# Two transformer-like blocks on one core: a narrower first query tile, norms behind a first unit, and a last layer begun on half its inputs

## What is computed

```
# first block
s = q . k over the allowed keys (causal: key <= query, dilated windows)   16 heads of 64
p = softmax(s); o = p @ v          # beside it a state-space branch
x = x + concat(attn, ssm) @ w_out
x = x + cross_attention(rms_norm(x, g_cross), rms_norm(mem, g_mem))
x = x + square(relu(rms_norm(x, g_mlp) @ w_up)) @ w_down
# second block
n = rms_norm(x, attn_norm) @ w_in  # MLA, 16 heads of 128+64, causal; an RG-LRU branch; gates
h = x + (g_attn * y_attn + g_rnn * y_rnn) @ w_out
# experts: per token and head the 16 best of 16384, 8 heads: 128 rows of 2048 from two tables
h = h + sum_k gate_k * gelu(u_k . rms_norm(h, ffn_norm)) * v_k
g = sigmoid(rms_norm(h, ple_norm) @ w_ple_gate); h = h + g * (p @ w_ple_proj)
out = rms_norm(h, final_norm)
```

## Time and profile before

| what | value |
|---|---|
| median of 3 runs | 3889.14 us (3883.0 to 3893.53) |
| profiled execution, own time | 3886.61 us |
| its span | 3884.6 us |
| PE busy | 3305.3 us, 85% |
| DVE busy | 2470.6 us, 64% |
| ACT busy | 1428.7 us, 37% |
| GpSimd busy | 847.1 us, 22% |
| DMA moved | 952.98 MB |

### The profile page before, as it was taken

The page is one execution under the profiler, slowest core; times in us unless marked ns, Lnnn a source line. Parts: engine busy times, 40 slices in busy tenths (PEclk is TensorE's granted clock), DMA queues, the critical chain, the costliest instruction groups (busy, mean ns, idle before and its releaser), DMA issues.

```text
span 3884.6 us, 53098 instructions
## 1 busy us (share of the span) xinstructions
PE 3305.3 (85%) x21008; PEld 2742.1 (71%) x21008; DVE 2470.6 (64%) x3257; ACT 1428.7 (37%) x2042; POOL 847.1 (22%) x623
## 2 busy tenths in 40 slices
PE   8988998999999999999999996766666666666688
PEld 8977887999999999999998996732222223222248
DVE  6567865654455556875546666977777776555556
ACT  6555555553345444564445452221000111000124
POOL 2000011000000100000000011255665565565522
PEclk9998999999999999999999997888888888888899
DMA  6423253555556565555552455899999999999964
GB/s 231 148 98 109 96 160 110 162 185 187 183 179 190 176 200 174 163 180 184 166 179 96 157 185 213 315 355 422 421 422 422 422 422 420 421 421 421 421 260 140
DMA packets 188023, 952.98 MB, mean 245 GB/s; under 512 B 20992, under 2 KB 20992, under 8 KB 121984
## 3 DMA queue, kind: packets, MB, share of 16 engines
q0 software_dynamic: 73728, 536.90, 33.6%
q1 hardware_dynamic: 114048, 412.70, 33.0%
HBM read 947.42 MB, written 2.10 MB: 244 GB/s over the span
## 4 chain that ended last, share of the span: by engine, by line
PE 58%; DMA 18%; DVE 13%; ACT 4%; POOL 4%; issue 2%; DVEq 0%; ACTq 0%; POOLq 0%; SPq 0%
PE ps L524 58%; DMA BIG<-in_peer_v,CS 6%; DMA HLF<-in_peer_v,CS 6%; DVE HL L1748 3%; DMA HF<-in_peer_v,CS 3%; DVE BIG L1752 2%; POOL HLF L506 2%; POOL BIG L506 2%; DMA BIG<-in_peer_u,CS 2%; DVE BIG L2390 1%; DMA HLF<-in_peer_u,CS 1%; DVE BIG L1748 1%; ACT BIG L1115 1%; ACT HL L1121 1%; PE ps L528 1%
## 5 line engine op out<-in xcount | busy, mean ns | idle before, releaser
L524 PE MATMUL ps<-HS,HL 128*128 128x256 f32 x10128 | 1344.8, 288 | 36.0 <-DVE HL L1748 29.9
L524 PEld LDWEIGHTS ps<-HS,HL 128*128 128x128 f32 x10128 | 1291.8, 196 | 47.5 <-DVE HL L1748 34.7
L1748 DVE TENSOR_TENSOR HL<-RAW,HL 128x1024 fp32r<-128x1024 f32 (+1 forms) x772 | 954.6, 1237 | 237.4 <-ACT HL L1121 174.1
L1121 ACT CAST HL<-RAW 128x1024 fp32r<-128x1024 f32 (+1 forms) x772 | 805.4, 1043 | 502.1 <-PE ps L524 454.4
L524 PE MATMUL ps<-BIGR,HL 128*128 128x256 f32 x6720 | 893.3, 284 | 24.2 <-DVE HL L1748 14.8
L524 PEld LDWEIGHTS ps<-BIGR,HL 128*128 128x128 f32 x6720 | 849.0, 192 | 32.2 <-issue 14.8
L524 PE MATMUL ps<-BIG,HF 128*128 128x512 f32 (+1 forms) x760 | 398.8, 675 | 191.2 <-DMA BIG<-in_peer_v,CS 168.1
L524 PE MATMUL ps<-HLF,HF 128*128 128x512 f32 x656 | 342.5, 674 | 154.2 <-DMA HLF<-in_peer_v,CS 140.6
L524 PEld LDWEIGHTS ps<-BIG,HF 128*128 128x128 f32 (+1 forms) x760 | 161.3, 222 | 423.3 <-issue 386.0
L473 POOL COPY NSUM<-TMP 128x256 f32<-128x256 f32 x6 | 3.3, 553 | 1957.6 <-ACT TMP L1117 1957.6
L2390 DVE CUSTOM_DVE_ANT_0 BIG<-BIG 128x2048 f32<-128x2048 f32 x133 | 305.0, 2293 | 167.3 <-DMA BIG<-in_peer_u,CS 158.1
(11 more groups left out here) (194 smaller groups left out, 2235.3 us busy)
## 6 DMA issues: line engine op xcount, KB each, us to landing
RAW<-in_w_up SPq DMA_DIRECT2D x128, 512.0 KB, 4.0
RAW<-in_w_down SPq DMA_DIRECT2D x128, 512.0 KB, 4.2
RAW<-in_w_out SPq DMA_DIRECT2D x64, 512.0 KB, 4.3
RAW<-in_w_qk SPq DMA_DIRECT2D x32, 512.0 KB, 3.4
RAW<-in_w_xbc SPq DMA_DIRECT2D x32, 512.0 KB, 3.5
RAW<-in_w_xr SPq DMA_DIRECT2D x32, 512.0 KB, 3.5
RAW<-in_w_yr SPq DMA_DIRECT2D x32, 512.0 KB, 3.8
RAW<-in_w_gr SPq DMA_DIRECT2D x32, 512.0 KB, 4.4
```

The lines of the kernel that those rows point to most:

```text
L524: return e.matmul(o, l, r, start=start, stop=stop, skip_group_check=True)
L1121: s.done(e.copy(o, i), sig)
L1748: v.done(e.tensor_tensor(o, a, b, op), sig)
```

## The change

1. Causal heads: the first tile's scores are taken over the first 128 keys alone. A head's scores are now 128 + 256 = 384 columns (`CAUSAL`), and so are the mask, the masking operation and the probabilities. The maxima take two reductions.
2. The four norm seams: PE's `norm_end` is called after the first unit of the next layer; ACT's makes a one-element root (`warm`) and `high(unit0 + 3)` ahead of its wait; DVE's makes `low(unit0 + 2)` and `low(unit0 + 3)` ahead of its wait.
3. Of the last 16 v rows DVE takes those with odd k, 8 instead of 4.
4. w2_pg is in `LATE`: its first three units need chunks 0 to 7 only. DVE's order of joining, adding, low halves and units is written anew, PE's first unit comes ahead of the last two half sums, ACT makes the third unit's high half ahead of the third half square, and the fourth's after the root.
5. Output: ACT multiplies each chunk of X by the gain into OUT inside the last layer; after the reciprocal DVE does four products of 1024 columns.

```
-LATE = ("w_ck", "w_out", "w2_ao")
+LATE = ("w_ck", "w_out", "w2_ao", "w2_pg")
+CAUSAL = ((0, 128), (128, 256))
...
         def by_vector(g):
-            return g[0] == "u" or g[2] % 4 == 3
+            return g[0] == "u" or g[2] % 4 == 3 or (g[1] == 15 and g[2] % 2 == 1)
...
# PE
-            def dense(L, src, evac=None, bg=None):
+            def dense(L, src, evac=None, bg=None, norm=None):
...
                         p.then_inc(s_mm, 1)
+                        if norm is not None and u == L.unit0:
+                            norm()
...
-                    for i in range(2):
-                        p = mm(b[:, i * T:i * T + T], QK[lo:lo + 64, c, i * 128:i * 128 + 128], QK[lo:lo + 64, 8 + c, :],
+                    for i, (at, w) in enumerate(CAUSAL):
+                        p = mm(b[:, at:at + w], QK[lo:lo + 64, c, i * 128:i * 128 + 128], QK[lo:lo + 64, 8 + c, 0:w],
...
-            norm_end("g_cross")
-            dense(L["w_cq"], normed("g_cross"), evac_cq, g_cr)
+            dense(L["w_cq"], normed("g_cross"), evac_cq, g_cr, lambda: norm_end("g_cross"))
...
-            half_sum(1, 2)
-            half_sum(1, 3)
-            dense(L["w2_pg"], cut_by(hg, s_nlo, lambda k: NORMED["ple_norm"] + k + 1))
+            def later_sums():
+                half_sum(1, 2)
+                half_sum(1, 3)
+            dense(L["w2_pg"], cut_by(hg, s_nlo, lambda k: NORMED["ple_norm"] + k + 1), None, None, later_sums)
...
# ACT
+            def warm():
+                act(WARM[:, :], con("ones")[:, 0:1], ACT.Sqrt)
-            def norm_end(name):
+            def norm_end(name, L=None):
+                if L is not None:
+                    warm()
+                    high(L.unit0 + 3)
                 s.wait_ge(s_nlo, NORMED[name] + 16)
                 rstd(name, 0, ADDED[name] + 1, RX, 2048, s_nsum)
...
             for j in range(4):
+                if j == 2:
+                    high(pg.unit0 + 2)
                 half_square(1, j)
...
                 squared("final", c)
-            high(pg.unit0 + 2)
+                act(OUT[:, c, :], X[:, c, :], ACT.Identity, (s_xg, c + 1), scale=vec("final_norm", c))
+            high(pg.unit0 + 3)
             dense(pg, evac_pg)
+            warm()
...
# DVE
             def norm_end(name, L=None):
                 normed_low(name, 15)
+                if L is not None:
+                    low(L.unit0 + 2)
+                    low(L.unit0 + 3)
                 v.wait_ge(s_nfree, NORM[name] + 1)
                 recip(RX, RX, (s_rx, RXN[name]))
...
+                stt(P[:, 0:384], score_bank(k)[:, 0:384], scale, con("mask"), ALU.mult, ALU.add, sig_score(k))
+                for i, (at, w) in enumerate(CAUSAL):
+                    total(d[:, i:i + 1], P[:, at:at + w], ALU.max, True, (s_max, n + 1) if i else None)
...
+            for b in range(3):
                 joined(1, b)
+            added(1, 0)
+            joined(1, 3)
+            added(1, 1)
+            low(pg)
+            normed_lows(0)
+            added(1, 2)
+            normed_lows(1)
+            low(pg + 1)
+            added(1, 3)
+            low(pg + 2)
+            normed_lows(2)
+            normed_lows(3)
+            low(pg + 3)
...
-            for c in range(16):
-                stt(OUT[:, c, :], X[:, c, :], vec("final_norm", c), RS[:, 0, :], ALU.mult, ALU.mult,
+            for i in range(4):
+                o = OUT[:, 4 * i:4 * i + 4, :]
+                tt(o, o, RS[:, 0, :].unsqueeze(1).to_broadcast([128, 4, T]), ALU.mult, (s_pout, i + 1))
```

More of the change, by code:

```diff
@@ L217, in build @@
         NSUM = sb("NSUM", [128, T])
+        WARM = sb("WARM", [128, 1])
         RX, CX = KEEP[:, 2, :], KEEP[:, 3, :]
@@ L649, in prepared, with softmax_head @@
                     yield
-            def softmax_head(name, h, score, P, PT, causal, vl, lo, rows, ahead=2):
+            def softmax_head(name, h, score, P, PT, vl, lo, rows, ahead=2):
                 k = SCORE[name] + (MLAH[h] if name == "mla" else h)
@@ L659, in softmax_head @@
                 pe.wait_ge(s_tfree, t)
-                for j, (i, c) in enumerate([(0, 0), (1, 0), (1, 1)] if causal else [(0, 0), (1, 0), (0, 1), (1, 1)]):
-                    p = tr(tr_bank[:, j * 128:j * 128 + 128], P[:, i * T + c * 128:i * T + c * 128 + 128])
+                for j in range(3):
+                    p = tr(tr_bank[:, j * 128:j * 128 + 128], P[:, j * 128:j * 128 + 128])
                 p.then_inc(s_turn, 1)
@@ L686, in attn @@
                     bank_done(L["w_v"], 7)
-                yield from softmax_head("attn", h, score, AP_[h % 4], APT, True,
+                yield from softmax_head("attn", h, score, AP_[h % 4], APT,
                                         lambda kt: VT[:, kt, h * 64:h * 64 + 64], lo, 64, 3)
@@ L982, in value @@
                     return V2[kt][:, h * 128:h * 128 + 128]
-                yield from softmax_head("mla", h, score, MP[h % 3], MPT, True, value, 0, 128)
+                yield from softmax_head("mla", h, score, MP[h % 3], MPT, value, 0, 128)
             g_ml = pipeline(mla(h) for h in range(16))
@@ L1036, in evac_pq @@
                 pq[0] = c + 1
-            dense(L["w_pq"], normed("ffn_norm"), evac_pq, beside())
+            dense(L["w_pq"], normed("ffn_norm"), evac_pq, beside(), lambda: norm_end("ffn_norm"))
             drain(g_sc)
@@ L1219, in prepared, with softmax_head @@
                     yield
-            def softmax_head(name, h, P, PT, scale, masked, causal, o, lo, rows, ahead=2):
-                k, n = SCORE[name] + (MLAH[h] if name == "mla" else h), HEAD[name] + h
+            def softmax_head(name, h, P, PT, o, lo, rows, ahead=2):
+                n = HEAD[name] + h
                 s.wait_ge(s_max, n + 1)
[L1224 to L1233, removed]
+                d = den(h)
+                for i, (at, w) in enumerate(CAUSAL):
+                    act(P[:, at:at + w], P[:, at:at + w], ACT.Exp, (s_exp, EXP[name] + h + 1) if i else None,
+                        bias=d[:, i:i + 1], acc=d[:, 2 + i:3 + i])
                 for _ in range(ahead):
                     yield
-                t, w = TURN[name] + h, 384 if causal else 512
+                t = TURN[name] + h
                 s.wait_ge(s_turn, t + 1)
@@ L1632, in scalar @@
             dense(L["w2_out"], residual("ffn_norm", L["w2_out"]))
-            norm_end("ffn_norm")
+            norm_end("ffn_norm", L["w_pq"])
             def rows():
@@ L2523, in constants @@
     m = ((d >= 0) & (d <= 128)).astype(int) + ((d >= 0) & (d % 4 == 0)) + ((d >= 0) & (d % 16 == 0))
-    c["mask"] = np.where(m > 0, np.log(np.maximum(m, 1)), NEG).reshape(128, 512)
+    c["mask"] = causal(np.where(m > 0, np.log(np.maximum(m, 1)), NEG))
     c["iota"] = np.broadcast_to(np.arange(16), (128, 16))
@@ L2540, in constants2 @@
     trig = np.stack([np.cos(ang), np.sin(ang)], axis=1).astype(np.float32)
-    return trig, np.where(d >= 0, 0.0, NEG).reshape(128, 512).astype(np.float32)
+    return trig, causal(np.where(d >= 0, 0.0, NEG)).astype(np.float32)
 def kernel(**inp):
```

95 lines of the change are left out of this document (37 added, 58 removed).

## The result

The changed kernel took 3862.7 us (median of 4 runs, 3859.9 to 3863.0) against 3887.9 us for the kernel before on the same chip (3883.0 to 3893.5): a ratio of 0.9933, 95% interval 0.9916 to 0.9950, so 0.7% faster, and clear of the spread. The forecast was 3856 with a range of 3844 to 3868. The time lies in the range and the direction was right, but the profiled span fell by 23.6 us (3884.6 to 3861.0) where the sum said 32.3.

The account below looks back on a forecast made before the run. TensorE was taken to bound the dense layers and DMA the expert gathers between them. Terms 3.0 + 6.7 + 13.2 + 6.2 + 3.2 = 32.3 us, from the median of 3889.14 to 3856.8, stated as 3856; range 3844 to 3868.

Parts of the forecast that it names:

- Narrow tile, attention: Attention stage: first query tile scored against 128 keys instead of 256 saves 3.0 us, bounds 1 to 4.5.
- Narrow tile, MLA: MLA stage: the narrower first-tile scores save TensorE 6.7 us, all taken as gain, bounds 4 to 7.5.
- Seams: Four norm seams: cross 2.6, MLP 3.0, attn_norm 5.1, ffn_norm 2.5; together 13.2 us, bounds 10 to 18.
- rival on the clock: The rival that the seams give the clock back: gain 36.5 us, up to 40, time 3851; chance 0.12.
- Rows: Last 16 expert rows: TensorE does 8 instead of 12, VectorE's joining starts at 3753.6; gain 3.75 us.
- the clock falls between the rows: Rival: TensorE's last eight expert rows run slow, and attention's chains surface; gain 24 us, time 3865; chance 0.17.
- the rows' stage absorbs it: Rival: the expert rows' stage ends at a fixed time, losing 22.9 us of earlier gains; time 3880; chance 0.03.
- Last layer: Last layer started on half its inputs: with the rows' 3.75 us a gain of 6.2, bounds 4.3 to 8.
- slower: Rival: the clock stays low through the last layer's 748 fast matmuls, ending 37 us slower, 3926; chance 0.02.
- Output: Kernel's end: sixteen VectorE products become four of 1024 columns; gain taken as 3.2 us, bounds 2.4 to 3.4.
- The seams give the clock back: Rival: no low clock at the seams; MLP gives 5.4 us, last layer up to 8; time 3851; chance 0.12.
- likeliest case: Whole kernel: the forecast itself, all terms together giving 32.3 us and a time of 3856; chance 0.66.

Follow-up runs that it names:

- both_wide: both_first, but MLA's first query tile scored against 256 keys on TensorE again; 3855.6 us, ratio 0.9923.
- both_first: The changed kernel with VectorE and TensorE serving MLA's newest live head first instead of the oldest; 3850.6 us, ratio 0.9908.
- fill_head12: The changed kernel with seven unused constant matmuls (3.0 us) on TensorE ahead of its wait at MLA's head 12; 3857.7 us, ratio 0.9925.
- seams_only: The kernel before with the four norm seam edits alone; 3876.7 us, ratio 0.9976.
- narrow_only: The kernel before with the narrow first query tiles of attention and MLA alone; 3877.4 us, ratio 0.9977.
- pe_first: The changed kernel with TensorE alone serving MLA's newest head first; 3858.2 us, ratio 0.9927.

## Why the prediction was right, and where it failed

**Narrow tile, attention.** Forecast 3.0. The pair of traces shows 2.0, ten executions with the narrow tile and three without differ by 4.3 on average at g_cross's last add (602.6 against 606.9). Inside my bounds of 1 to 4.5, and not to be had more exactly: this stretch differs by up to 2.5 us between executions of like code.

**Narrow tile, MLA.** This is the step that failed: "In MLA PE waited 1.7 us in 200, so I take all 6.7." The size of PE's saving was right (0.42 us a head, and both_wide against both_first gives 6.70). But the wait was read as a small remainder of idle, and so as proof that PE is the bound. It was the opposite: the one place where PE's lead over a slower ring comes due. PE had run ahead of the ring by 0.2 us a head for the whole stage; making it faster by 0.42 only spent the lead sooner. The ring itself gained 0.19 us a head, 3 us in all, and the wait grew from 1.74 to 3.26. Then the clock fell and took 3.8 us more, so that MLA gave -1.2 us from the first value product to the last (91.97 to 93.18), and 0.0 from its first score. With the clock kept up (fill_head12) the same stretch takes 105.4 us against 109.3. So of the 6.7 us the clock took 3.9 and the ring kept back 2.8. I had written that "a chain through DVE and ACT may surface", but with a lower bound of 4, where nothing was possible; and of the clock only in other places.

**Seams.** Forecast 13.2; 13.3 in seams_only. In the changed kernel cross gave 3.7 instead of 2.6: PE's first scores of cross came 2.2 us sooner, counted from g_cross's last add, and they ran at the full clock, where the kernel before had the low one. PE's timeline, before and changed:

```profile
633.50 2.04 PE L524 MATMUL ps<-BIG 128*128 128x256 f32 x4 [1.29 <-DVE BIG L1748]
...
629.30 1.10 PE L529 MATMUL ps<-BIG 128*128 128x256 f32 x4 [1.29 <-DVE BIG L1755]
```

This isn't chance: these matmuls take 1.10 us in all ten kernels with the seam edit and 2.04 or 2.05 in the three without, and the whole stretch 84.3 to 85.5 us against 88.4 to 89.1. It belongs to my rival on the clock. The low clock moved more than it went: it was at 0.50 from 632.9 to 639.7 and again from 653.4 to 660.2 us in the kernel before, from 641.5 to 655.2 in the changed one. attn_norm gave about 4.3 instead of 5.1: its first four units met no idle, but the fifth waited 0.89 us for its low, where I had no wait. The MLP gave 2.6 instead of 3.0. So the sum agrees because the misses cancel. The 2.98 us of idle at the MLP and the place of the reciprocal ahead of the routing came as forecast. DVE's reciprocal of ffn_norm at 2330.34 is 12.5 us sooner than in the earlier trace rows, the transposes 15.2.

**Rows.** Forecast 3.75, found 3.7 in all nine kernels that have the edit. Of PE's eight last rows in the changed kernel six followed 1.15 to 1.31 us of idle and took 3.67 us; the first followed 3.79 us of idle and was slow, as in the kernel before, and the second came behind it without idle, which the forecast's "eight PE rows" with 1.3 us of idle overlooked. The rival "the clock falls between the rows" is refuted. So is "the rows' stage absorbs it": from the routing's transposes to DVE's last row it took 1393.0 to 1396.6 us wherever it began, from 2329 to 2357 us. One count of mine was short: over the whole stage of the kernel before 60 rows, not 35, followed 3.77 us of idle or more; all of them were slow.

**Last layer.** Forecast 2.45, found 2.1. The waits that I had laid out came where I had put them: for the fourth half sum's square (1.27 us) and for the fifth low (1.72). The rival "slower", with the clock low in the last layer, didn't occur; from 3748 us it is 1.00.

**Output.** Forecast 3.2, found 3.1.

**The seams give the clock back** came true in part: the sum's matmul takes 0.60 us at three seams, at two of which (attn_norm and ffn_norm) it had taken 1.22, and cross ran faster than forecast. But the clock that was lost at MLA's end is more than what was given back.

So the likeliest case was right in all terms but one; taking out its 7.5 us leaves a gain of 24.8 and a forecast of 3864.3 on the median's scale, where 3862.7 was measured. The range held because it reached to the low ends of the bounds.

## What to carry to other kernels

In a stage that several engines pass work round in turn, measure the pace of each: the time from one head to the next of one operation on each engine, and how the distance between two engines' operations drifts along the stage. A single wait at the stage's end, small against the stage, doesn't show that the waiting engine is the bound; where the distance shrinks steadily, it isn't. There, speeding up the engine that is ahead buys nothing until the order within the ring is changed (here newest first on two engines, 9.9 us), and then it pays in full.

When an edit is worth less than what two executions differ by, compare the stretch that it touches, and keep a list of the stretches that it doesn't: narrow_only's total agreed with my forecast to 0.1 us and nearly half of it came from code that was the same.

## What the hardware showed

The granted clock fell to 0.50 at a wait of PE of 3.26, 3.27, 3.02 and 2.05 us at MLA's end (five kernels), and stayed at 1.00 at 1.74 and 1.75 us there (two kernels). Two things speak against the wait's length as the whole rule: pe_first's clock fell at a wait of 1.69 us (its windows are at 0.78 and 0.88), and in the kernel before, a row after 2.09 us of idle in the gathers' stage ran at full speed. What decides wasn't tried. Nor is a fall worth the same each time: with the same work behind it, the product after the wait's came 10.48 us later in the changed kernel and 7.61 in narrow_only, against 6.64 in the kernel before. The clock was at 0.50 for about 10.2 us in the first (2129.7 to 2140.0) and 3.4 in the second (2138.5 to 2141.9). The Trainium skill ("TensorE: Matmul & The Clock Gate", section "HAM oscillation") warns of bursts with waits between them that begin at half rate. The rule that I had weighed for the last rows, where it didn't come true behind 1.15 to 1.31 us of idle, describes MLA's end in the changed kernel, where fill_head12 prices it at 3.9 us.
